# Gate projections by seven half-block products, with weight sums on GpSimd, in a hybrid attention and mixture-of-experts block

## What is computed

```
h    = rmsnorm(x, norm1_g)
proj = h @ w_in + b_in                       # 1024 -> 4352 columns
qa, ka, va, qb, kb, vb, ga, gb = split(proj) # ga, gb: 1024 columns each
oa = neighborhood_attention(qa, ka, va, rpb) # 8 heads
ob = sliding_window_gqa(rope(qb), rope(kb), vb, sinks)   # 8 heads
merged = sigmoid(ga) * (oa @ w_up_a) + sigmoid(gb) * (ob @ w_up_b)
x = x + merged @ w_out
x = x + moe(rmsnorm(x, norm2_g))             # top 4 of 32 experts, weights 32 x 12 MB
return rmsnorm(x, final_g)
```

## Time and the profile before

| | |
|---|---|
| Median of 3 runs | 1134.62 us (1134.04 to 1134.88) |
| Profiled execution, its own time | 1134.65 us |
| Its span from first to last instruction | 1132.8 us |
| Mean granted TensorE clock | 0.997 of full |
| TensorE busy | 1077.8 us, 95% |
| VectorE busy | 285.9 us, 25% |
| ScalarE busy | 104.2 us, 9% |
| GpSimd busy | 11.2 us, 1% |

### The profile page before, as it was taken

One profiled execution on the slowest core, in us unless ns is written; L12 is line 12 of the kernel. 1 busy time (PEld: TensorE's weight loads), 2 busy tenths in 40 slices (PEclk: granted clock), 3 DMA queues, 4 the chain that ended last, 5 costly groups with the idle time before them and its releaser, 6 DMA issues.

```text
span 1132.8 us, 13083 instructions
## 1 busy us (share of the span) xinstructions
PE 1077.8 (95%) x5173; PEld 477.6 (42%) x5173; DVE 285.9 (25%) x614; ACT 104.2 (9%) x221; POOL 11.2 (1%) x20
## 2 busy tenths in 40 slices
PE   8999999999999999999999999999999999999997
PEld 7888788633333333333333333333333333333332
DVE  4346412322222222222222222221211122222222
ACT  1130430200000000000000000000000000000001
POOL 1100000000000000000000000000000000000000
PEclk9999999999999999999999999999999999999999
DMA  9954257589999999999999999999999999999995
GB/s 357 420 220 148 85 213 333 200 350 429 427 428 429 429 428 429 428 429 428 429 428 429 428 429 429 428 429 428 429 429 429 428 429 428 429 428 429 428 425 231
DMA packets 34917, 436.35 MB, mean 385 GB/s; under 512 B 4336, under 2 KB 4848, under 8 KB 6896
## 3 DMA queue, kind: packets, MB, share of 16 engines
q1 hardware_dynamic: 33888, 435.10, 91.4%
q10 hardware_dynamic: 1008, 0.95, 0.2%
HBM read 434.98 MB, written 1.05 MB: 385 GB/s over the span
## 4 chain that ended last, share of the span: by engine, by line
PE 74%; DMA 18%; SPq 4%; DVE 3%; issue 1%; another core or an unknown queue 0%; ACT 0%; POOL 0%; POOLq 0%; DVEq 0%
PE bank L777 29%; DMA ring<-in_w 17%; PE bank L810 15%; PE bank L504 8%; PE bank L693 4%; PE bank L743 4%; SPq L349 4%; PE bank L699 3%; PE bank L618 2%; PE bank L600 2%; DVE work L1140 1%; PE bank L500 1%; PE bank L761 1%; PE bank L459 1%; PE bank L524 1%; PE bank L553 1%
## 5 line engine op out<-in xcount | busy, mean ns | idle before, releaser
L777 PE MATMUL bank<-ring,work 128*64 128x512 f32 x2048 | 450.9, 593 | 21.2 <-DMA ring<-in_w 20.6
L777 PEld LDWEIGHTS bank<-ring,work 128*64 128x64 f32 x2048 | 147.3, 137 | 304.1 <-issue 273.8
L810 PE MATMUL bank<-ring,work 128*64 128x512 f32 x1024 | 233.6, 598 | 18.1 <-DVE work L1140 18.1
L810 PEld LDWEIGHTS bank<-ring,work 128*64 128x64 f32 x1024 | 67.9, 136 | 141.1 <-issue 115.4
L1131 DVE TENSOR_SCALAR work<-bank 128x512 f32<-128x512 f32 x32 | 22.1, 692 | 415.5 <-PE bank L777 415.5
L504 PE MATMUL bank<-ring 128*128 128x256 f32 x432 | 96.5, 381 | 0.0
L1270 ACT ACTIVATE work<-work 128x512 f32<-128x512 f32 x32 | 20.1, 629 | 754.0 <-DVE work L1131 754.0
L504 PEld LDWEIGHTS bank<-ring 128*128 128x128 f32 x432 | 81.1, 190 | 13.2 <-issue 2.4
L693 PE MATMUL bank<-x2n,work 128*64 128x512 f32 x264 | 65.0, 614 | 0.8 <-DVE work L1047 0.8
L743 PE MATMUL bank<-work 64*128 64x512 f32 x256 | 63.6, 615 | 0.9 <-DVE work L1145 0.9
L1067 DVE TENSOR_TENSOR work<-bank,vec 128x256 f32<-128x256 f32 x64 | 24.2, 420 | 136.5 <-PE bank L699 136.5
(11 more groups left out here) (176 smaller groups left out, 447.1 us busy)
## 6 DMA issues: line engine op xcount, KB each, us to landing
ring<-in_w SPq DMA_DIRECT2D x190, 2048.0 KB, 40.3
ring<-in_w_in SPq DMA_DIRECT2D x16, 1024.0 KB, 24.4
ring<-in_w_out SPq DMA_DIRECT2D x4, 1024.0 KB, 4.7
ring<-in_w SPq DMA_DIRECT2D x3, 1024.0 KB, 45.9
ring<-in_w_up_a SPq DMA_DIRECT2D x2, 1024.0 KB, 10.0
ring<-in_w_up_b SPq DMA_DIRECT2D x2, 1024.0 KB, 6.8
ring<-in_na_rpb SPq DMA_DIRECT2D x1, 1536.0 KB, 19.1
ring<-in_w SPq DMA_DIRECT2D x2, 512.0 KB, 39.7
```

Of the source, the lines that this page charges most:

```text
L777: last = pe.matmul(bank[CAP * a:CAP * (a + 1), bk, :], kT, pairs[:, pair_of(par, k // 2), at + q * 512:at + (q + 1) * 512], start=False, s ...
L810: last = pe.matmul(bank[CAP * a:CAP * (a + 1), BH, :], fT, pairs[:, pair_of(par, c), at + a * 512:at + (a + 1) * 512], start=f == 0, stop= ...
```

## The change

The eight gate chunks are computed by another formula. A chunk's weights are seen as four half blocks `w_block(c, kh, a)` (half of the depth `kh`, column block `a`; four slices of 128x128), the activations as four half blocks `h_block(kh, m)` (half of the depth, token tile `m`). A 2 by 2 product of blocks, which takes eight block products, is done with seven (the Winograd form of Strassen's method), each of four matmuls with 128 tokens moving.

- **GpSimd**: `weight_sums(c)`, four additions or subtractions of 128x512 for each gate chunk, each after the one before it; they begin when unit 3's maxima are done (`max_ready` is 4), and from chunk 11 on after chunk `c - 2` is used.
- **VectorE**: `sum_tokens()` once, four such sums of the activations, after `softmax_back(3)`; `mix_first(c)` (five operations on 128x128 from PSUM) and `mix_second(c)` (three) for each gate chunk. In chunk 10 they stand around the last operation of the b1 split, ahead of `rotary`.
- **TensorE**: `gate_products(c, 0)` (four products), then `turn_probs` of that chunk, which now stands in the middle, then `gate_products(c, 1)` (three products). Each part has its own PSUM bank, taken in turn out of three.
- **ScalarE**: `read_gates` is gone; the sigmoid is done in two pieces after the last chunk. In the gate chunks `exponentials` now stands ahead of `read_probs`.

The diff, cut to its core:

```diff
+        w_sums = tables.rearrange("p (i n k c) -> p i n k c", i=2, n=3, k=4)
+        h_sums = arena[:, q_at:q_at + 8 * T].rearrange("p (n k t) -> p n k t", n=4, k=4)
+        mixed = cut(2048, 4 * P).rearrange("p (n t) -> p n t", n=4)
...
+            def weight_sums(c):
+
+                n, s = c - GATE_C, w_sums[:, c % 2]
+                pool.wait_ge(landed[slot_of(c)], landings(c))
+                if n >= 2:
+                    pool.wait_ge(chunk_used, c - 1)
+                pool.tensor_tensor(s[:, 0], w_block(c, 0, 0), w_block(c, 0, 1), ALU.subtract).then_inc(w_sum_ready, 1)
+                pool.wait_ge(w_sum_ready, 4 * n + 1)
+                pool.tensor_tensor(w_block(c, 0, 1), w_block(c, 0, 1), w_block(c, 1, 1), ALU.add).then_inc(w_sum_ready, 1)
+                pool.wait_ge(w_sum_ready, 4 * n + 2)
+                pool.tensor_tensor(s[:, 1], w_block(c, 0, 1), w_block(c, 0, 0), ALU.subtract).then_inc(w_sum_ready, 1)
+                pool.wait_ge(w_sum_ready, 4 * n + 3)
+                pool.tensor_tensor(s[:, 2], w_block(c, 1, 0), s[:, 1], ALU.subtract).then_inc(w_sum_ready, 1)
+
+            pool.wait_ge(max_ready, 4)
+            for c in range(GATE_C, N_IN):
+                weight_sums(c)
...
+            def product(dst, a, b):
+
+                for k in range(4):
+                    last = pe.matmul(dst, a[:, k, :], b[:, k, :], start=k == 0, stop=k == 3)
+                return last
+
+            def gate_products(c, part):
...
+                if phase < 3:
+                    pe.wait_ge(proj_read_dve, GATE_C - 2 + phase)
+                else:
+                    pe.wait_ge(gate_part_read, phase - 2)
+                dst = quarter(gate_bank(c, part))
+                if part == 0:
+                    pe.wait_ge(landed[slot_of(c)], landings(c))
+                    product(dst[:, 0, :], w_block(c, 0, 0), h_block(0, 0))
+                    if n == 0:
+                        pe.wait_ge(h_sums_ready, 4)
+                    pe.wait_ge(w_sum_ready, 4 * n + 1)
+                    product(dst[:, 1, :], s[:, 0], h_sums[:, 2])
+                    pe.wait_ge(w_sum_ready, 4 * n + 2)
+                    product(dst[:, 2, :], w_block(c, 0, 1), h_sums[:, 0])
+                    pe.wait_ge(w_sum_ready, 4 * n + 3)
+                    product(dst[:, 3, :], s[:, 1], h_sums[:, 1]).then_inc(gate_half_done, 1)
+                else:
+                    product(dst[:, 0, :], w_block(c, 1, 0), h_block(1, 0))
+                    product(dst[:, 1, :], w_block(c, 1, 1), h_sums[:, 3])
+                    pe.wait_ge(w_sum_ready, 4 * n + 4)
+                    product(dst[:, 2, :], s[:, 2], h_block(1, 1)).then_inc(chunk_used, 1)
...
-                if turned is not None:
+                if turned is not None and c < GATE_C:
                     turn_probs(turned)
                 if scored is not None:
                     scores(scored)
-                if c:
+                if c >= GATE_C:
+                    gate_products(c, 0)
+                    if turned is not None:
+                        turn_probs(turned)
+                    gate_products(c, 1)
+                elif c:
                     project(c)
...
+            def sum_tokens():
+
+                dve.tensor_tensor(h_sums[:, 2], h_block(1, 1), h_block(0, 1), ALU.subtract).then_inc(h_sums_ready, 1)
+                dve.tensor_tensor(h_sums[:, 0], h_block(0, 1), h_block(0, 0), ALU.subtract).then_inc(h_sums_ready, 1)
+                dve.wait_ge(h_sums_ready, 2)
+                dve.tensor_tensor(h_sums[:, 1], h_block(1, 1), h_sums[:, 0], ALU.subtract).then_inc(h_sums_ready, 1)
+                dve.wait_ge(h_sums_ready, 3)
+                dve.tensor_tensor(h_sums[:, 3], h_sums[:, 1], h_block(1, 0), ALU.subtract).then_inc(h_sums_ready, 1)
...
+                if c >= GATE_C and c != ROPE_C:
+                    mix_first(c)
                 if scored is not None:
                     softmax_back(scored)
+                if c == GATE_C - 1:
+                    sum_tokens()
+                if c >= GATE_C and c != ROPE_C:
+                    mix_second(c)
...
                     ch.link(dve.tensor_tensor(b1_raw[low, :], b1_raw[low, :], b1_parts[low, :], ALU.subtract))
+                    mix_first(c)
                     dve.tensor_copy(b1_parts[low, :], b1_raw[low, :]).then_inc(b1_split, 1)
+                    mix_second(c)
+                    dve.wait_ge(gate_part_read, 2 * (c - GATE_C + 1))
                     rotary()
...
-            for c in range(N_IN + 1):
+            for c in range(N_IN):
                 turned, scored = unit_at(TURN_C, c), unit_at(UNIT_C, c)
+                if c >= GATE_C and scored is not None:
+                    exponentials(scored)
                 if turned is not None:
                     read_probs(turned)
-                if c > GATE_C:
-                    read_gates(c - 1)
-                if scored is not None:
+                if c < GATE_C and scored is not None:
                     exponentials(scored)
```

More of the change, by code:

```diff
@@ L170, in build_block @@
         pick = cut(3072, 128).rearrange("p (m s) -> p m s", m=MT)
+        q_at = left[0]
         qaT = attn_buf(4 * T).rearrange("p (b t) -> p b t", t=T)
@@ L253, in build_block @@
         msq_ready, rstd_ready = sem("msq_ready"), sem("rstd_ready")
-        proj_read_dve, proj_read_act = sem("proj_read_dve"), sem("proj_read_act")
+        proj_read_dve, gate_part_read = sem("proj_read_dve"), sem("gate_part_read")
+        w_sum_ready, h_sums_ready, gate_half_done = sem("w_sum_ready"), sem("h_sums_ready"), sem("gate_half_done")
         masked_bias, rope_done, rope_ready = sem("masked_bias"), sem("rope_done"), sem("rope_ready")
@@ L307, in build_block @@
         unit_at = lambda table, c: table.index(c) if c in table else None
-        LAST_PLAIN = TURN_C[-1]
         BS, BT, BO, BK = 3, 5, 7, 3
@@ L321, in bcast, with w_block, h_block, gate_bank @@
             return bass.AP(v.tensor, at, [[0, P], [1, n]])
+        def w_block(c, kh, a):
+            w = ring[:, slot_of(c), :].rearrange("p (k n) -> p k n", n=CW)
+            return w[:, 4 * kh:4 * kh + 4, a * P:(a + 1) * P]
+        def h_block(kh, m):
+            return hT[:, 4 * kh:4 * kh + 4, m * P:(m + 1) * P]
+        def gate_bank(c, part):
+            return (2 * (c - GATE_C) + part) % 3
         def projected(c, a):
@@ L480, in project @@
                 if c >= 3:
[L482 to L485, removed]
+                    pe.wait_ge(proj_read_dve, c - 2)
                 w = ring[:, slot_of(c), :].rearrange("p (k n) -> p k n", n=CW)
@@ L510, in project @@
                 last.then_inc(chunk_used, 1)
+            def product(dst, a, b):
[3 more added lines that the diff above has]
+            def gate_products(c, part):
+                n, s = c - GATE_C, w_sums[:, c % 2]
+                phase = 2 * n + part
+                if phase < 3:
[19 more added lines that the diff above has]
+                    product(dst[:, 2, :], s[:, 2], h_block(1, 1)).then_inc(chunk_used, 1)
             def scores(u):
@@ L592, in _ @@
                     pe.wait_ge(o_ready, UNITS)
-                    pe.wait_ge(proj_read_act, N_IN - 2 - GATE_C)
+                    pe.wait_ge(gate_part_read, 2 * (N_IN - GATE_C) - 1)
                 if n == 2:
-                    pe.wait_ge(proj_read_act, N_IN - GATE_C)
+                    pe.wait_ge(gate_part_read, 2 * (N_IN - GATE_C))
                 w = ring[:, slot_of(c), :].rearrange("p (k n) -> p k n", n=512)
@@ L955, in read_output, with gate_of, mix_first, mix_second @@
                 dve.tensor_copy(oT[:, u, :], bank[:, BO, 0:T]).then_inc(o_ready, 1)
+            def sum_tokens():
[5 more added lines that the diff above has]
+                dve.tensor_tensor(h_sums[:, 3], h_sums[:, 1], h_block(1, 0), ALU.subtract).then_inc(h_sums_ready, 1)
+            def gate_of(c, a, m):
+                return gates[:, 2 * (c - GATE_C) + a, m * P:(m + 1) * P]
+            def mix_first(c):
+                dve.wait_ge(gate_half_done, c - GATE_C + 1)
+                m1, m7, m5, m6 = (quarter(gate_bank(c, 0))[:, q, :] for q in range(4))
+                bias = [vec[:, 2 * c + a:2 * c + a + 1] for a in range(2)]
+                dve.wait_ge(gate_part_read, 2 * (c - GATE_C))
+                if c == ROPE_C + 1:
+                    dve.wait_ge(rope_ready, 1)
+                ch.link(dve.tensor_copy(mixed[:, 0], m1))
+                ch.link(dve.tensor_tensor(mixed[:, 1], m6, mixed[:, 0], ALU.add))
+                dve.scalar_tensor_tensor(out=mixed[:, 2], in0=m5, scalar=bias[0], in1=mixed[:, 1], op0=ALU.add, op1=ALU.add)
+                ch.link(dve.scalar_tensor_tensor(out=mixed[:, 3], in0=m7, scalar=bias[1], in1=mixed[:, 1],
+                                                 op0=ALU.add, op1=ALU.add))
+                dve.tensor_tensor(gate_of(c, 1, 1), m5, mixed[:, 3], ALU.add).then_inc(gate_part_read, 1)
+            def mix_second(c):
```

(21 more changed lines are left out.)

## The result

The changed kernel takes 1148.2 us (1147.68 to 1148.84, 4 runs), the kernel before 1134.33 us in 4 runs: a ratio of 1.0125, 95% interval 1.0113 to 1.0136. It is slower by 13.9 us. The forecast was 1150, range 1136 to 1155.

The account below looks back on a forecast made before the run. TensorE (95% busy) and memory (428 GB/s) are both full; the expert-weight stream sets the end. Upward projections start at 172.4 instead of 156.8 us, 15.6 later: 1134.65 + 15.6 = 1150 us, range 1136 to 1155.

Parts of the forecast that it names:

- The bound: Whole kernel: the stream of expert weights sets the end, which moves with the start of the upward projections, 15.6 us later.
- The port: VectorE beside GpSimd: an SBUF-only operation, two-input additions included, waits for the whole GpSimd operation; 1.70 us for a pair.
- Rival A: VectorE beside GpSimd: only single-input operations such as casts wait, additions of two SBUF tensors don't; 1136.8 us, chance 0.17.
- Rival B: Gate stage: no engine waits for another's port, the b1 path alone is late, `scores(4)` by 2.3 us; 1133.8 us, chance 0.12.
- Rival C: Ahead of `scores(4)`: b1 and rotary don't matter and TensorE keeps its 5.7 us gain; 1129 us, chance 0.07.
- Step 1: Chunk 9: VectorE's token sums take turns with GpSimd until 88.8 us, so TensorE waits 5.5 us for them.
- Step 2: b1 loads go out at 92.7 us instead of 83.59; the split's five operations wait 5.2 us beside GpSimd; split and mixing end at 115.5.
- Step 3: Rotary: three operations wait beside GpSimd's sums for chunk 13, 2.5 us; `scores(4)` starts 15.4 us later.
- Step 4: `scores(4)` to upward projections: 47.9 us, less 3.8, plus 4.3 for VectorE's mixing and waits for ScalarE's copies; they start at 172.4.
- The products: TensorE, gate chunks: 56 instructions in 6.3 us instead of 7.01 per chunk; eight chunks give back 5.7 us.

Follow-up runs that it names:

- memset run: Changed kernel with each GpSimd weight sum replaced by a memset of the same 128x512 area, weight sums left out; one execution, 1138.2 us.
- thin run: Changed kernel with all GpSimd weight sums taken over one column in 128, so the gates are wrong; 1135.82 us, ratio 1.0009.
- versions with plain chunks: Changed kernel with plain products in chunks 9 to 11, seven products from chunk 12, GpSimd's sums later: 1133.97 us; with two repairs 1131.6 us.
- version with two repairs: Plain-chunks version, plus GpSimd's sums for chunks 14 to 16 waiting for probabilities and ScalarE copying first in chunk 13; 1131.6 us, ratio 0.9979.

## Why the prediction was right

**The bound.** The end moved with the start of the upward projections: 15.4 us there and 14.1 at the experts, counted from `attend(2)`, and 13.5 in the span, which contains the 0.9 by which this trace runs ahead. The forecast had 15.6. One reading of the earlier trace rows was off without bearing on the sum: memory is at 425 to 429 GB/s from the tenth slice to the last but one, three quarters of the span and not over four fifths.

**The port.** The step that decided, that an addition of two SBUF tensors waits like L894, held: 1.63 to 1.75 us instead of 0.69, a pair in 1.67 (forecast 1.70). The 0.55 us that VectorE needs after the GpSimd operation's end was met too (84.49 after 83.94), though 0.69 less the 0.20 read from L894 is 0.49. The waiting goes both ways: the GpSimd operation that comes later ends later, 1.59 to 3.19 us instead of 1.27. The Trainium skill's rule in SBUF — State Buffer, section "Who interferes with whom", that a VectorE instruction with two SBUF inputs contends with a GpSimd instruction that reads SBUF, agrees with these rows. The Trainium skill also says there that such an instruction doesn't contend with a GpSimd operation that only writes, and the memset run agrees (0.69 beside memsets). Rival A (only casts wait) is out by these rows. Rival B (no engine waits for another's port) is out by them too; the thin run comes close to what it would have been. Rival C, that b1 and rotary don't matter, is out by TensorE's wait of 6.69 us for the end of rotary.

**Step 1, the token sums.** Forecast a wait of 5.5 us, measured 5.13. GpSimd took 1.27 per operation (1.3).

**Step 2, b1.** The loads were to go out 11.3 us after `attend(2)`; they did 12.7 after. What was missing is the clock: the three products behind the wait took 4.3 us instead of 2.7. The landing took 5.9 us (5.6). The split's five operations took 12.9 us: 4.5 of waits, where 5.2 were forecast.

**Step 3, rotary.** 9.0 us, so 2.9 of waits (2.5). `scores(4)` is 16.8 us later, forecast 15.4.

**Step 4, the rest.** This was wrong in its parts and 1.6 us too long in its sum. Forecast: 4.3 us of waits for ScalarE's copies. Measured: one, of 0.55, ahead of `attend(4)`. In its place came the clock: 9.31 us from `scores(4)` to `scores(5)` instead of 7.51, 1.8 lost. Together 46.5 us, against 48.1 forecast and 44.05 without either. In chunk 12 there was nothing to hold VectorE: GpSimd was idle from 124.2 to 134.3 us, and unit 4's maximum (0.17 us) and its two multiplications (1.29) kept their plain lengths. The mechanism of the copies behind the exponentials was real all the same: it appeared in the versions with plain chunks (2.06 and 1.88 us), where `softmax_back` or the maximum had run beside GpSimd.

**The products.** 56 instructions in 6.3 to 6.4 us, as worked out from L508. Chunk 10, which nothing held up, took 6.35 us instead of 7.01. By that, eight chunks would give 5.3 us (an estimate; the forecast had 5.7), and from `scores(4)` on, with chunks 12 to 16, 3.8 are measured when nothing waits.

The forecast left TensorE's clock out. On the path it cost about 1.6 us in chunk 9 and 1.8 after `scores(4)`; the slow stretch at 113.71 lay beside rotary and cost nothing. That it nearly made up for the waits of step 4 that didn't come was luck: up to `scores(4)` the forecast was 1.4 us short, behind it 1.6 us long, and the two cancel in the 15.6.

## What to carry to other kernels

Work given to an idle GpSimd isn't free for VectorE: before moving it, list VectorE's operations that run in SBUF alone (two tensor inputs, casts, and single-input operations such as L894) in the same stretch, and price each pair at nearly the sum of both (here 1.67 us for 0.69 and 1.27). Place GpSimd's work beside VectorE's PSUM reads or in its idle time; here that, a shorter reach of the new formula and ScalarE's copies ahead of the exponentials turned 14 us lost into 4 us gained. Where a wait of TensorE is repaired, look one chunk on, and count what its clock loses after every wait of some microseconds.

## What the runs showed of the hardware

In this stage of the eleven traces, waits of TensorE of 1.9 to 9.1 us were each followed by a stretch at a mean granted clock of 0.54 to 0.79 (0.56 after the wait of 1.88 us, 0.54 after 2.06, 0.63 after 5.13, 0.70 after 9.08); 24 instructions took 4.4 us instead of 2.84. The clock also moved where nothing was changed: ahead of the first expert, behind the same two waits of 1.42 and 0.83 us, it was at 0.66 before and at 1.00 after, worth 1.2 us.

Even operations of a few elements are held up beside GpSimd. In the version with two repairs, a `TENSOR_SCALAR` on 128x4 beside GpSimd took 1.13 us instead of 0.17; it is the one that releases the exponentials:

```profile
120.31 1.09 DVE L1013 TENSOR_TENSOR mx<-mx,sink_b 128x4 f32<-128x4 f32 x1
...
121.62 1.13 DVE L1015 TENSOR_SCALAR neg_mx<-mx 128x4 f32<-128x4 f32 x1
```
